# A two-block transformer kernel: weights held in the MLP's later slices, bias rows in parts, low parts of heads a step later, seven sets of scan tables

## The reference, cut to what matters

```python
def first_block(x, c, ...):            # i = 0, then 1
    for i in range(2):
        shift, scale, gate = modulation(silu(c), mod_mix_w[i], mod_mix_b[i])
        h = x * (1 + scale) + shift
        y = mla_mixer(h, ...) if i == 0 else s5_mixer(h, ...)
        x = layer_norm(ALPHA * x + (1 + gate) * y, ...)
        shift, scale, gate = modulation(silu(c), mod_ffn_w[i], mod_ffn_b[i])
        h = x * (1 + scale) + shift
        y = square(relu(h @ w1[i] + b1[i])) @ w2[i] + b2[i]     # 1024 -> 4096 -> 1024
        x = layer_norm(ALPHA * x + (1 + gate) * y, ...)

def second_block(x, ...):              # l = 0, then 1
    for l in range(2):
        x = macaron_ffn(x)             # (silu(x w_gate) * (x w_up)) w_down, inner width 2816
        xn = rms_norm(x, ...)
        m = recurrent_block(xn) if l == 0 else attention(xn, k, v, rel_bias) @ w_o
        x = x + rms_norm(m, ...)
        x = macaron_ffn(x)
        if l == 0: k, v = split(rms_norm(x) @ w_kv)
```

## Time and profile before

| what | value |
|---|---|
| median of 3 executions | 1749.22 us |
| profiled execution | 1750.2 us, its span 1748.6 us |
| PE busy | 1646.2 us, 94% |
| DVE, ACT busy | 66%, 48% |
| TensorE clock granted, mean | 0.969 |
| HBM | 192 GB/s over the span |

### The profile page before, as it was taken

The page is one execution under the profiler, slowest core; times in us unless marked ns, Lnnn a source line. Parts: engine busy times, 40 slices in busy tenths (PEclk is TensorE's granted clock), DMA queues, the critical chain, the costliest instruction groups (busy, mean ns, idle before and its releaser), DMA issues.

```text
span 1748.6 us, 20517 instructions
## 1 busy us (share of the span) xinstructions
PE 1646.2 (94%) x8221; PEld 1327.7 (76%) x8221; DVE 1147.3 (66%) x1354; ACT 839.1 (48%) x1134; POOL 153.8 (9%) x293
## 2 busy tenths in 40 slices
PE   7778999988988999999999999999999999799998
PEld 3656787875677788878888868888788888578887
DVE  4699778888969665575546876544754546665554
ACT  3553465544234555544335875334634435553433
POOL 4510100026600100000000000000000000000000
PEclk9878999999999999999999989999999999899999
DMA  9838588752036566445654554555555554245551
GB/s 305 310 126 308 185 302 332 288 214 100 1 142 220 193 227 238 161 168 192 225 184 141 199 189 171 192 192 169 207 178 183 186 188 167 96 144 193 193 191 74
DMA packets 145096, 335.45 MB, mean 192 GB/s; under 512 B 18213, under 2 KB 34061, under 8 KB 143850
## 3 DMA queue, kind: packets, MB, share of 16 engines
q1 hardware_dynamic: 134310, 293.65, 48.8%
q0 software_dynamic: 9696, 37.29, 5.6%
q10 hardware_dynamic: 996, 3.20, 0.5%
HBM read 328.86 MB, written 6.83 MB: 192 GB/s over the span
## 4 chain that ended last, share of the span: by engine, by line
PE 71%; DVE 16%; ACT 5%; issue 4%; POOL 2%; DMA 1%; SPq 1%; DVEq 0%; ACTq 0%; POOLq 0%
PE ps L670 22%; PE ps L672 22%; PE ps L671 22%; DVE wlo L1794 3%; PE ps L755 2%; ACT whi L1253 1%; DMA operands<-in_mod_mix_w 1%; PE ps L749 1%; DVE work L2247 1%; DVE xlo L1799 1%; PE ps L762 1%; DVE B L1927 1%; POOL mod L2509 1%; DVE B L1926 1%; DVE small L1859 1%
## 5 line engine op out<-in xcount | busy, mean ns | idle before, releaser
L1794 DVE TENSOR_TENSOR wlo<-raw,whi 128x2048 fp32r<-128x2048 f32 (+2 forms) x247 | 559.8, 2283 | 253.5 <-ACT whi L1253 252.2
L1253 ACT ACTIVATE whi<-raw 128x2048 fp32r<-128x2048 f32 (+2 forms) x247 | 466.9, 1908 | 233.9 <-PE ps L672 170.5
L670 PE MATMUL ps<-whi,xhi 128*128 128x512 f32 (+2 forms) x1244 | 477.5, 384 | 18.9 <-DVE xlo L1799 17.3
L672 PE MATMUL ps<-whi,xlo 128*128 128x512 f32 (+2 forms) x1244 | 471.8, 379 | 0.0
L671 PE MATMUL ps<-wlo,xhi 128*128 128x512 f32 (+2 forms) x1244 | 471.7, 379 | 0.0
L670 PE MATMUL ps<-whi,hhi 128*128 128x512 f32 x736 | 294.6, 400 | 6.2 <-DVE hlo L1799 5.2
L671 PE MATMUL ps<-wlo,hhi 128*128 128x512 f32 x736 | 289.0, 393 | 0.0
L672 PE MATMUL ps<-whi,hlo 128*128 128x512 f32 x736 | 288.8, 392 | 0.0
L670 PEld LDWEIGHTS ps<-whi,xhi 128*128 128x128 f32 x1244 | 235.5, 189 | 64.6 <-DVE xlo L1799 21.0
L672 PEld LDWEIGHTS ps<-whi,xlo 128*128 128x128 f32 x1244 | 235.5, 189 | 44.2
L671 PEld LDWEIGHTS ps<-wlo,xhi 128*128 128x128 f32 x1244 | 235.8, 190 | 41.7
(11 more groups left out here) (371 smaller groups left out, 1599.8 us busy)
## 6 DMA issues: line engine op xcount, KB each, us to landing
raw<-in_mlp_w SPq DMA_DIRECT2D x64, 1024.0 KB, 5.6
raw<-in_ffn_w_gate SPq DMA_DIRECT2D x44, 1024.0 KB, 5.1
raw<-in_ffn_w_up SPq DMA_DIRECT2D x44, 1024.0 KB, 5.2
raw<-in_ffn_w_down SPq DMA_DIRECT2D x44, 1024.0 KB, 4.9
mod<-in_mod_ffn_w POOLq DMA_DIRECT2D x16, 1024.0 KB, 6.9
mod<-in_mod_mix_w POOLq DMA_DIRECT2D x12, 1024.0 KB, 7.4
operands<-in_mod_mix_w SPq DMA_DIRECT2D x8, 1024.0 KB, 8.5
raw<-in_lru_w_in SPq DMA_DIRECT2D x8, 1024.0 KB, 5.2
```

Source lines behind the costliest of these rows:

```text
L670: pe.matmul(o, lh, rh, start=start, stop=False)
L672: return pe.matmul(o, ll, rh, start=False, stop=stop)
L1253: act.activation(whi[:, c % SPL, 0:n], raw[:, c % RAW, 0:n], ACT.Copy).then_inc(hi_done, 1)
L1794: dve.tensor_tensor(wlo[:, c % RAW, 0:n], raw[:, c % RAW, 0:n], whi[:, c % SPL, 0:n].bitcast(F32), ALU.subtract).then_inc(lo_done, 1)
```

## The change

- MLP, up chunks of slices 2 to 7: shape COLS instead of HALF, weights stationary and 256 tokens moving. The result has hidden units on partitions already: no copy for the turn, no turn. ACT's `hidden_features` applies relu and bias straight from PSUM (two 128 x 256 pieces per chunk) and squares; DVE's part has the same size, by chunk instead of by token tile.
- MLP, bias row b2: no `open_acc`. ACT makes a high part (`brow_hi`) and DVE a low part (`brow_lo`); `down` of slice 0 begins each of its four sums with two fp32r matmuls of one row.
- MLP, residual stream: behind the hidden units of slice 0, after the third and fourth low part of that slice.
- Attention, both: the multiplications with the reciprocal move from DVE to ACT (Copy with a scale per partition), the low part of a head's output comes one head later. MLA: the rotary turn of the second half and the wait for its queries move into heads 0 and 2, and the work beside the heads comes one head later. Att: the scores of heads 0 and 1 come before the second token tile of the last projection, head 2 after it; the queries of heads 4 to 7 are copied after ACT's first exp.
- S5: seven sets of tables instead of three. The first gate chunk in two halves, each waiting for its half of `xhi`, `xlo`. gelu's wait goes by another semaphore.
- LRU: `open_acc` before `turned(3)`.

```diff
 SLICES = {"mlp0": 8, "s5": 2, "mlp1": 8, "ffn10": 6, "lru": 4, "ffn20": 6, "kv": 4, "ffn11": 6, "att": 2, "ffn21": 6}
-TURNED = {n: (2 if n == "kv" else k) for n, k in SLICES.items()}
+TURNED = {n: (2 if n in ("kv", "mlp0", "mlp1") else k) for n, k in SLICES.items()}
...
+        elif name in ("mlp0", "mlp1"):
+            for k in range(3, n - 3):
+                both(c + k, c + k + 1) if k >= 6 and k % 4 > 1 else each(c + k, c + k + 1)
...
-                    chunks[mlp_up(name, i, h)] = (up_src(t["mlp_w1"][l], i, h), HALF)
+                    chunks[mlp_up(name, i, h)] = (up_src(t["mlp_w1"][l], i, h), HALF) if i < 2 else (ws_src(t["mlp_w1"][l], 2 * i + h), COLS)
...
-            def down(c, tile, tt, first=False, final=False, src=(hhi, hlo)):
+            def down(c, tile, tt, first=False, final=False, src=(hhi, hlo), biased=None):
...
                     for n in range(2):
+                        if biased and k == 0:
+                            half = slice(512 * n, 512 * (n + 1))
+                            pe.matmul(ps[:, 2 * tt + n, :], ones_r[0:1, :], brow_hi[:, half], start=True, stop=False)
+                            last = pe.matmul(ps[:, 2 * tt + n, :], ones_r[0:1, :], brow_lo[biased][:, half], start=False, stop=False)
+                            if tt and n:
...
                 elif name in MLPS:
-                    if j == 1:
-                        pe.wait_ge(hid_ok, HID0[name] + 14 + tt + 1)
+                    if j:
+                        pe.wait_ge(hid_ok, HID0[name] + 14 + j)
...
                     if i:
+                        columns(mlp_up(name, i + 1, 0), slice_bank(i + 1, 0))
+                    if i < 2:
                         for tt in range(T):
-                            project(name, mlp_up(name, i + 1, 0), slice_bank(i + 1, tt), tt, 0)
+                            token_turn(name, i, tt)
+                    if i:
+                        columns(mlp_up(name, i + 1, 1), slice_bank(i + 1, 1))
+                    else:
+                        for tt in range(T):
+                            project(name, mlp_up(name, 1, 1), slice_bank(1, tt), tt, 1)
                     for tt in range(T):
-                        token_turn(name, i, tt)
-                    for tt in range(T):
-                        project(name, mlp_up(name, i + 1, 1), slice_bank(i + 1, tt), tt, 1)
-                    if i == 0:
-                        open_acc(name)
-                    for tt in range(T):
-                        pe.wait_ge(hid_ok, HID0[name] + 2 * i + tt + 1)
-                        down(mlp_down(name, i, 0), 4 * (i % 2), tt)
-                        if i == 6 and tt == 0:
-                            for t2 in range(T):
-                                token_turn(name, 7, t2)
+                        if i == 0:
+                            acc_ready(name, tt)
+                            pe.wait_ge(brow_lo_ok, MLPS.index(name) + 1)
+                        pe.wait_ge(hid_ok, HID0[name] + 2 * i + (tt if i < 2 else 0) + 1)
+                        down(mlp_down(name, i, 0), 4 * (i % 2), tt, biased=name if i == 0 else None)
+                    pe.wait_ge(hid_ok, HID0[name] + 2 * i + 2)
...
+                    if g:
+                        turn_rotary(0)
...
-                for g in range(2):
-                    pe.wait_ge(qp_ok, g + 1)
-                    for r in range(2):
-                        for tt in range(T):
-                            last = pe.transpose(ps[:, 4 * g + 3, r * L + tt * P:r * L + (tt + 1) * P], qp_tok[:, g, tt, r * P:(r + 1) * P], ident[:, :])
-                    last.then_inc(qt_ps, 1)
-                pe.wait_ge(q_ok, 4)
-                pe.wait_ge(qt_ok, 2)
+                pe.wait_ge(q_ok, 2)
+                pe.wait_ge(qt_ok, 1)
...
             def beside_attention(i):
-                if i == 1:
+                if i == 0:
+                    turn_rotary(1)
+                if i == 2:
+                    pe.wait_ge(q_ok, 4)
+                    pe.wait_ge(qt_ok, 2)
                     same_step()
-                if i == 2:
+                if i == 3:
...
-                if i == 4:
...
+            def attention(n, q, k, v, rotary, scored=0):
...
                 for i in range(HEADS + 3):
-                    if i < HEADS:
...
+                    if scored <= i < HEADS:
+                        if n and i == 4:
+                            pe.wait_ge(feat_ok, FEAT0["att"] + 4)
+                        scores(n, i, q, k, rotary)
...
-                pe.wait_ge(g_ok, 2)
-                for j in range(4):
+                chunk_ready(c + 4)
+                wh, wl = parts(c + 4, COLS)
+                for hf in range(2):
+                    pe.wait_ge(g_ok, hf + 1)
+                    for m in range(2):
+                        for k in range(4 * hf, 4 * hf + 4):
+                            last = mm3(ps[:, 4 * (1 - m), m * L:(m + 1) * L], wh[:, k, m * P:(m + 1) * P], wl[:, k, m * P:(m + 1) * P],
+                                       xhi[:, k, :], xlo[:, k, :], k == 0, k == KT - 1)
...
+                for j in range(1, 4):
...
-                turned(3)
...
                 open_acc("lru")
+                turned(3)
...
-                for tt in range(T):
-                    project("att", c + 3, slice_bank(1, tt), tt, 1)
+                project("att", c + 3, slice_bank(1, 0), 0, 1)
+                acc_ready("att", 1)
+                pe.wait_ge(feat_ok, FEAT0["att"] + 2)
+                scores(1, 0, qT2, kT2, False)
+                scores(1, 1, qT2, kT2, False)
+                project("att", c + 3, slice_bank(1, 1), 1, 1)
+                scores(1, 2, qT2, kT2, False)
...
-                acc_ready("att", 1)
-                pe.wait_ge(feat_ok, FEAT0["att"] + 4)
-                attention(1, qT2, kT2, V2, False)
+                attention(1, qT2, kT2, V2, False, scored=3)
...
+                def hidden_features(i, b):
+                    act.wait_ge(pe_pass, passed(mlp_up(name, i, b)))
+                    act.wait_ge(hid_ok, h + 2 * (i - 1) + b + 1)
+                    r = TMP[:, 1024 + 512 * b:1536 + 512 * b]
+                    for j in range(2):
+                        n = 32 * l + 4 * i + 2 * b + j
+                        steps.did(act.activation(r[:, j * L:(j + 1) * L], ps[:, 4 + 2 * (i % 2) + b, j * L:(j + 1) * L],
+                                                 ACT.Relu, bias=b1c[:, n:n + 1]))
+                    steps.settle()
+                    act.activation(hhi[:, 4 * (i % 2) + 2 * b:4 * (i % 2) + 2 * b + 2, :], r.rearrange("p (k n) -> p k n", k=2),
+                                   ACT.Square).then_inc(hid_hi, 1)
                 def hidden(i, tt):
+                    if i >= 2:
+                        hidden_features(i, tt)
+                        return
...
+                if l == 0:
+                    act.activation(ones_r[:, :], ones[0:1, :], ACT.Copy)
+                act.wait_ge(brow_in, 16 * (l + 1))
+                act.activation(brow_hi[:, :], brow[name], ACT.Copy).then_inc(brow_hi_ok, 1)
...
                     for tt in range(T):
-                        token_copy(name, i + 1, tt, mlp_up(name, i + 1, 1))
+                        if i == 0:
+                            token_copy(name, 1, tt, mlp_up(name, 1, 1))
...
                     act.activation(qpT[:, 2 * g:2 * g + 2, :].rearrange("p r l -> p (r l)"), ps[:, 4 * g + 3, :], ACT.Copy).then_inc(qt_ok, 1)
-                hi(5)
+                    if g == 0:
+                        hi(5)
...
+                        if n and i == 0:
+                            for tt in range(T):
+                                feature_copy("att", 1, tt, qT2)
+                    if 1 <= i <= HEADS:
+                        s = (i - 1) % 3
+                        act.wait_ge(rc_ok, HEADS * n + i)
+                        for tt, (lo, up) in enumerate(((0, P), (P, 3 * P))):
+                            last = act.activation(sms[:, s, lo:up], sms[:, s, lo:up], ACT.Copy, scale=recips[:, 2 * s + tt:2 * s + tt + 1])
+                        last.then_inc(p_ok, 1)
...
                 def table(i):
-                    s = i % 3
+                    tab = tabs[i % 7]
                     act.wait_ge(phase_r, i + 1)
...
-                        act.wait_ge(x_rot, i - 2)
-                    act.activation(tabs[:, s, 1, :], ph[:, i % 2, 0, :], ACT.Sin, scale=TWO_PI * (1 - 2.0 ** -22))
+                    if i >= 7:
+                        act.wait_ge(x_rot, i - 6)
+                    act.activation(tab[:, 1, :], ph[:, i % 2, 0, :], ACT.Sin, scale=TWO_PI * (1 - 2.0 ** -22))
...
-                    act.activation(tabs[:, s, 0, :], half, ACT.Copy, scale=-2.0, bias=1.0).then_inc(table_ok, 1)
+                    act.activation(tab[:, 0, :], half, ACT.Copy, scale=-2.0, bias=1.0).then_inc(table_ok, 1)
...
+                for tt in range(T):
+                    feature_copy("att", 0, tt, qT2)
                 hi(c + 5)
```

(34 more changed lines are left out.)

88 lines of the change are left out of this document (52 added, 36 removed).

## The result

The changed kernel takes 1725.78 us (median of 4 runs, 1721.54 to 1727.38) against 1749.33 before (4 runs, 1749.03 to 1751.65): ratio 0.9859, 95% interval 0.9839 to 0.9879. The forecast was 1720, range 1708 to 1733. The profiled execution took 1721.54, its span is 1719.8: the lowest of its four runs.

What follows compares the result with a forecast made beforehand. PE was taken to bound the long stages, the chain over DVE and ACT the attentions. Terms -13.6 (mlp0 and mlp1), -5.5, -5.5, +0.5, -5.5 sum to -29.6: profiled 1750.2 becomes 1720.6, forecast 1720, range 1708 to 1733.

Steps and rivals of the forecast that it cites:

- Part 2: MLPs, bias row in parts and residual stream later: -5.0 us in mlp0, -3.4 in mlp1, together -8.4, bounds -4 and -9.7.
- Part 1: MLPs, weights held in slices 2 to 7, fewer turns but 0.120 us matmuls: -1.5 us per MLP, -3.0 for both.
- Part 3: Mlp0, PE's waits for low parts go because the token copies delaying ACT go: -2.2 us, bounds 0 and -2.6.
- Part 4: S5, seven table sets end DVE's waits for POOL and half the gate chunk starts earlier: -5.5 us, bounds -1.5 and -6.5.
- Part 7: Att, earlier first scores -1.5 us, multiplication and low part out of the ring -4.0: sum -5.5, bounds -2 and -8.
- Part 5: MLA heads, earlier scores for head 0 and multiplications moved from DVE to ACT: -5.5 us, bounds -1 and -9.
- Rival A: Attentions give little, heads staying bound by DVE's other work and half clock, or ACT late for PE: 1731 us; chance 0.23.
- Part 6: LRU, bias row fills PE's wait, but PE then idles some 5 us before the first product: +0.5 us, bounds -1.4 and +2.

Runs made afterwards that it cites:

- best: Changed kernel with att's multiplications on DVE, lru's bias row behind the last turns, and the MLPs' eight bias matmuls together before the hidden-unit wait: 1718.77 us, ratio 0.9810.
- after: The changed kernel without further edit, first profile: profiled execution 1721.54 us.
- again: The changed kernel once more, no edit, second profile: its series of five runs gave 1726.16 us, ratio 0.9852.
- open_acc: Changed kernel with eight fp32 one-row bias matmuls back before slice 0's first down chunk in both MLPs, residual stream still late: 1729.24 us, ratio 0.9872.
- tables3: Changed kernel with three sets of tables instead of seven in s5: 1729.47 us, ratio 0.9877.

## Why the prediction was right, step by step

The whole was right: -23.6 in the medians, -28.7 between the profiled executions (1750.2 to 1721.5), against -29.6. The 5 us between the two come from the choice of the execution: the one that was profiled is the shortest of its four. That the sum is so near has luck in it: part 2 was too large by 3.5 us, parts 1 and 3 together and part 4 too small by about as much, and part 7 was right for a wrong reason.

- **Part 1, right.** 0.120 us per matmul and 22.42 per iteration (forecast 22.4). With held weights a late transfer made PE wait in mlp1 in eight of eleven traces (0.33 to 1.86 us), though not in the first, and in mlp0 in best alone; ACT now waits for chunks in mlp0 46.7 us in all, before 11.1.
- **Part 3, right in mechanism, too small.** The rest of mlp0 gave 6.3 where parts 1 and 3 had 3.7, and all of it goes back with the tokens held. In the two traces PE's waits in this stretch fell from 4.7 to 1.3 us: 2.6 that I had named (2.2 taken), and 0.8 of the last one (2.14, now 1.33) that I had not. The matmuls beside the three small waits were late as well, some 0.3 per wait, which with the one at 369.76 is 0.9 to 1.0. And PE's own stream gave 2.0 instead of 1.5, since a pair of turns costs 0.89 and the one that is left, between matmuls of 256 columns, only 0.55.
- **Part 2, the step that was mis-sized.** -8.4 forecast, -4.9 to -5.1 measured. "The new bias matmuls are 8 of 512 columns: 8 x 0.227 = 1.8" is wrong: between full matmuls a pair costs 0.66 and its neighbours are late too.

```profile
192.87 0.40 PE L688 MATMUL ps<-whi,hlo 128*128 128x512 f32 x1
193.19 0.49 PE L734 MATMUL ps<-brow_hi,ones_r 1*128 1x512 f32 x1
193.53 0.39 PE L735 MATMUL ps<-brow_lo,ones_r 1*128 1x512 f32 x1
193.85 0.50 PE L686 MATMUL ps<-whi,hhi 128*128 128x512 f32 x1
194.19 0.39 PE L687 MATMUL ps<-wlo,hhi 128*128 128x512 f32 x1
```

  From 192.87 to 194.19 it is 1.32 where two full matmuls take 0.46: 0.86 per pair, 3.4 for four, nearly the old row's 3.7. With that 1.6 more, PE's wait of 0.62 for the low part that I had at nothing, and none of the 0.6 that I kept for the clock, the forecast of -5.0 for mlp0 becomes -3.4; measured are -3.1 and -3.4. For mlp1 the same corrections make -2.0 of -3.4, and -1.7 is measured. (That DVE was idle for over 15 us between 210 and 231 is misread: it was 12.8.) The two halves of the part also depend on each other: late residual with the old row saves 2.7 and 0.5, the new row on top 0.6 and 1.3, the new row with the early residual costs 5.4 and 6.5 against the kernel before. I had put the residual down as cover for the bias row and not priced the row as cover for the residual.
- **Part 4, right in mechanism, somewhat too small.** -6.9 for -5.5: the tables 3.9 (forecast 3.2), the gate's first half 2.2 (its wait 4.10 became 1.89, forecast 2.3). The 0.8 that is left goes with less half clock in s5 (10 us against 17), which no run here separates.
- **Part 5, right in direction, the clock decides the size.** -4.3 in the first trace, -7.4 or some -3.5 in the others, against -5.5. The multiplications give 2.2 to 6.3 (forecast 3.9). Head 0's scores, forecast to come 3.6 earlier than at 82.62, came at 83.25, 80.49 and 78.31 (after, again, best). Rival A had PE's half clock take part of this, and it did in three of ten traces.
- **Part 6, right in sign.** +0.2 to +1.6, forecast +0.5. The wait of some 5 us came, but behind the first down chunks instead of before the first product, and the matmul behind it took 0.80. The Trainium skill (TensorE: Matmul & The Clock Gate, Part 1) has it that an idle engine falls back to half clock; the trace agrees behind the wait of 5.11 us, while the matmul behind the one of 1.41 took 0.47, at full clock.
- **Part 7, right sum, wrong cause: luck.** -5.5 for -5.5. "With multiplication and low part out of it, ACT's own work is the bound" holds for every second head only (2.2 us, no wait); the others take 3.2 with a wait of 0.8 to 1.0 for DVE, and the multiplication is 2.6 better on DVE. What broke the ring is the low part alone, 5.1 in the kernel before; the early scores gave 2.1, and the multiplications on ACT took 2.6 back. The three don't add up to 5.5 exactly, as each was measured with the others in a different state.

The Trainium skill (ScalarE: Activation LUTs, rules for kernel authors) keeps plain multiplications off ACT. Att agrees, with 2.6 us; MLA does not, where DVE works 24.8 of 26 us and the same move wins 2.2 to 6.3. The rule prices the instruction, and the chain decides which engine pays.

What stays open: why the clock fell behind mlp0's bias matmuls in best and not behind mlp1's; why the transfers of mlp0 came later in that trace; and where the changed kernel's runs at a clock of 0.975 lose their time, since no profile has one of them.

## What to carry to other kernels

In a software pipeline over three engines, look first for the instruction that stands ahead of the next item's first step on an in-order queue and waits for the last item's end; moving that one back by an item was worth 5.1 us in att, where the work taken off DVE lost 2.6. In MLA, where DVE is full, the same move did nothing. Two edits that hide each other (a long bias row, a late residual) must be priced together and apart. And where PE waits anyway, look whether the wait stands in one piece: of two traces with the same code, the one with a wait of 5.18 us in MLA's heads had half clock on the 28 matmuls behind it and came out 3.9 us longer.

## What the runs showed of the hardware

Matmuls with one row of operands cost more between full ones than their 512 columns say: 0.43 each there, against (194.52 - 192.79)/7 = 0.25 in a row of eight. Eight fp32 matmuls of one row take 3.7 us at full clock (192.72 in open_acc) and 7.19 at half. The changed kernel scatters by 9 us from run to run in 1720, and in it the time goes with the granted clock, 1.8 us per 0.001; in the kernel before and in tables3 it does so weakly or not at all. Part of the scatter is a transfer of mlp1 that lands up to 2.4 us later in one trace than in another (28.8 and 31.2 us behind slice 0) and costs PE up to 1.9 us. The kernel before had 2.6 us in its first series, but 1748.2 to 1755.1 over the later ones.
